# A feed-forward norm whose per-token scale moves behind the first product, with the tokens' parts made beside the output matrix, in a two-block model kernel on one core

## The reference, cut to what matters

```python
def rms_norm(x, g):
    y = xf * lax.rsqrt(jnp.mean(xf * xf, axis=-1, keepdims=True) + RMS_EPS)
    return (y * g.astype(jnp.float32)).astype(x.dtype)

def conv_glu_ffn(h, w_up, conv_w, w_down):
    up = causal_dwconv(h @ w_up, conv_w)          # three taps along the tokens, per channel
    gate, val = jnp.split(up, 2, axis=-1)
    return (jax.nn.silu(gate) * val) @ w_down     # D_FF = 2816

    # in first_block
    x = x + hybrid_mixer(...)                     # ends in: merged @ w_o
    h = rms_norm(x, ffn_norm_g[l])
    x = x + conv_glu_ffn(h, w_up[l], ffn_conv_w[l], w_down[l])
```

## Time and profile before

| what | us |
|---|---|
| runs | 1736.82, 1743.10, 1745.94 |
| median of the runs | 1743.10 |
| profiled execution, first to last instruction | 1743.0 |
| TensorE busy in it | 1663.4 (95%) |
| VectorE, ScalarE, GpSimd busy | 1147.6, 800.3, 347.2 |
| branch products (L933) begin | 301.86 |
| last product of the output matrix begins | 354.94 |
| first product of the feed-forward part (L1098) begins | 374.23 |
| last `down` ends, about | 565.2 |

### The profile page before, as it was taken

One profiled execution on the slowest core, in us unless ns is written; L12 is line 12 of the kernel. 1 busy time (PEld: TensorE's weight loads), 2 busy tenths in 40 slices (PEclk: granted clock), 3 DMA queues, 4 the chain that ended last, 5 costly groups with the idle time before them and its releaser, 6 DMA issues. The chain is left out here.

```text
span 1743.0 us, 32776 instructions
## 1 busy us (share of the span) xinstructions
PE 1663.4 (95%) x11200; PEld 1507.4 (86%) x11200; DVE 1147.6 (66%) x2258; ACT 800.3 (46%) x1331; POOL 347.2 (20%) x220
## 2 busy tenths in 40 slices
PE   4999998969999999999999998999999999999997
PEld 4987897859999977778999998999999888888886
DVE  4454423757777594661679994777775577777776
ACT  3442111345554463223355554555555455555554
POOL 0030000004444000335667995000000000000000
PEclk9999998989999999999999999999999999999999
DMA  6513222335554521114645786555556767666663
GB/s 229 191 39 108 75 87 98 132 120 181 185 188 169 195 86 49 49 37 172 203 152 187 221 230 190 178 178 172 179 177 201 227 231 239 232 231 229 235 238 123
DMA packets 92804, 289.44 MB, mean 166 GB/s; under 512 B 10304, under 2 KB 27072, under 8 KB 92352
## 3 DMA queue, kind: packets, MB, share of 16 engines
q1 hardware_dynamic: 92304, 287.61, 50.6%
q10 hardware_dynamic: 432, 0.90, 0.2%
HBM read 270.64 MB, written 17.83 MB: 166 GB/s over the span
## 5 line engine op out<-in xcount | busy, mean ns | idle before, releaser
L259 PE MATMUL psum<-arena_parts 128*128 128x256 f32 (+2 forms) x1664 | 477.2, 287 | 26.2 <-DVE ring_parts L254 12.3
L261 PE MATMUL psum<-arena_parts,ring_parts 128*128 128x256 f32 (+1 forms) x1600 | 450.4, 282 | 0.0
L2589 DVE TENSOR_TENSOR ring_parts<-ring,arena_parts 128x512 fp32r<-128x512 f32 x418 | 282.7, 690 | 122.5 <-ACT arena_parts L2389 98.8
L259 PEld LDWEIGHTS psum<-arena_parts 128*128 128x128 f32 x1664 | 316.0, 190 | 29.8 <-issue 22.0
L261 PEld LDWEIGHTS psum<-arena_parts,ring_parts 128*128 128x128 f32 x1600 | 303.6, 190 | 0.0
L260 PE MATMUL psum<-h_parts,arena_parts 128*128 128x256 f32 x1024 | 287.2, 280 | 0.0
L254 POOL TENSOR_TENSOR ring_parts<-ring,arena_parts 128x1024 fp32r<-128x1024 f32 x79 | 210.2, 2681 | 65.2 <-ACT arena_parts L250 48.0
L230 PE MATMUL psum<-h,ring 128*128 128x256 f32 x896 | 212.5, 397 | 0.0
L2358 PE MATMUL psum<-arena_parts,x_parts 128*128 128x512 f32 x512 | 206.1, 403 | 2.7 <-DVE x_parts L2616 2.7
L2360 PE MATMUL psum<-arena_parts,x_parts 128*128 128x512 f32 x512 | 202.7, 396 | 0.0
L2359 PE MATMUL psum<-ring_parts,x_parts 128*128 128x512 f32 x512 | 202.0, 395 | 0.0
(11 more groups left out here) (527 smaller groups left out, 2924.2 us busy)
## 6 DMA issues: line engine op xcount, KB each, us to landing
ring<-stream SPq DMA_DIRECT2D x473, 512.0 KB, 3.5
kept<-arena SPq DMA_DIRECT2D x128, 128.0 KB, 2.6
arena<-kept SPq DMA_DIRECT2D x32, 512.0 KB, 4.2
arena<-first SPq DMA_DIRECT2D x1, 2144.0 KB, 7.8
arena<-second SPq DMA_DIRECT2D x1, 1632.0 KB, 6.4
x<-x_t SPq DMA_DIRECT2D x1, 1024.0 KB, 5.7
out<-arena SPq DMA_DIRECT2D x4, 256.0 KB, 2.1
arena<-last ACTq DMA_DIRECT2D x1, 512.0 KB, 3.4
```

Of the source, the lines that this page charges most:

```text
L259: nc.tensor.matmul(dst, stationary[0], moving[0], start=first, stop=False)
L261: return nc.tensor.matmul(dst, stationary[1], moving[0], start=False, stop=last_one)
L2589: v.tensor_tensor(low[:, s, w], ring[:, s, w], expert_high[:, m % 2, w].bitcast(F32), ALU.subtract)\
```

## The change

- The merge and the feed-forward part are one block: no meeting of the engines between them, and none around a norm.
- While the output matrix is multiplied, as each tile of `x` is done, ScalarE makes `h_high` as the rounded `x` times the gain (no scale of the token) and the tile's square; VectorE makes `h_low` from `x`, the gain and `h_high` by one instruction (`x_low`). GpSimd adds the squares in pairs.
- TensorE multiplies by the identity straight behind the output matrix, then by ones, and goes on with `up`.
- The scale of the tokens is made while the first `up` runs. It is put on the products: `scale_up` multiplies a bank by `scale` into a new tile in SBUF, `up_scaled`, and `up_taken` says that the bank is free. `convolve` then reads `up_scaled`.
- The last two slots of `W_O` change places, so that slot 3, which `FF_FIRST` needs, comes free one block earlier.

```diff
-        W_O = (4, 5, 6, 7, 0, 1, 2, 3)
+        W_O = (4, 5, 6, 7, 0, 1, 3, 2)
...
+        up_scaled = a6.take(2, 2, T)
...
-        rms_norm(lambda k: x[:, k, :], lambda k: h[:, k, 0:T], "ffn_norm_g", RMS_EPS, squares,
-                 beside=(lambda act: [ff_high(act, n) for n in (-4, -3)], lambda dve: [ff_low(dve, n) for n in (-4, -3)]))
...
+                for k in range(KT):
+                    b = k % 4
+                    act.wait_ge(drained[b], ev_at.banks[b] + k // 4 + 4)
+                    nc.scalar.activation(h_high[:, k, :], x[:, k, :], ACT.Identity, scale=col("ffn_norm_g", k))\
+                        .then_inc(S("h_rounded"), 1)
+                    nc.scalar.activation(squares[:, k, 0:T], x[:, k, :], ACT.Square).then_inc(S("scalar_step"), 1)
+                    if k in (5, 6):
+                        ff_high(act, k - 9)
+                sca.n += KT
+                ff_high(act, -2)
...
+            @block.gpsimd
+            def _(pool):
+                for k in range(4):
+                    pool.wait_ge(S("scalar_step"), sca.n - 3 + k)
+                    nc.gpsimd.tensor_tensor(squares[:, 4 + k, 0:T], squares[:, 4 + k, 0:T], squares[:, k, 0:T], ALU.add)\
+                        .then_inc(S("norm_squares"), 1)
...
+                def x_low(k):
+                    dve.wait_ge(S("h_rounded"), split["h"] + k + 1)
+                    v.scalar_tensor_tensor(h_low[:, k, :], x[:, k, :], col("ffn_norm_g", k), h_high[:, k, :].bitcast(F32),
+                                           ALU.mult, ALU.subtract).then_inc(S("h_parts"), 1)
...
+                for k in range(4):
+                    pe.wait_ge(S("norm_squares"), normed["squares"] + k + 1)
+                    ins = mm(bank[7][:, 0:T], ones, squares[:, 4 + k, 0:T], start=k == 0, stop=k == 3)
+                ins.then_inc(S("norm_total"), 1)
...
-                        pe.wait_ge(S("up_read"), i * 2 + (j + 1))
+                        pe.wait_ge(up_taken, i * 4 + (2 * j + 2))
...
+                        if n + part == -1:
+                            pe.wait_ge(S("norm_mean"), n_norm + 1)
...
-                            src, dst, c = bank[4 + 2 * j + part], conv[:, j, part, :], i * 2 + (j + FT * part)
+                            src, dst, c = up_scaled[:, j, part, :], conv[:, j, part, :], i * 2 + (j + FT * part)
...
+                        v.tensor_tensor(up_scaled[:, j, part, :], bank[4 + 2 * j + part][:, 0:T], scale[:, 0:T], ALU.mult)\
+                            .then_inc(up_taken, 1)
...
+                dve.wait_ge(S("norm_total"), n_norm + 1)
+                vec.link(v.tensor_scalar(scale[:, 0:T], bank[7][:, 0:T], 1.0 / D, RMS_EPS, ALU.mult, ALU.add))
+                vec.tell(v.reciprocal(scale[:, 0:T], scale[:, 0:T]), S("norm_mean"), n_norm + 1)
+                ff_low(dve, -1)
+                dve.wait_ge(S("norm_root"), n_norm + 1)
                 with dve.Fori(0, pairs) as i:
                     for j in range(2):
                         ff_low(dve, 3 * j, i)
+                        scale_up(i, j)
                         ff_low(dve, 3 * j + 1, i)
                         convolve(i, j)
                         ff_low(dve, 3 * j + 2, i)
                 for j in range(2):
                     ff_low(dve, j, pairs)
                 for j in range(2):
+                    scale_up(pairs, j)
                     convolve(pairs, j)
```

More of the change, by code:

```diff
@@ L918, in build, with ff_block, ff_high, ff_low @@
         merged_sum, merged_rounded = S("gn_squares"), S("gn_inverse")
+        a6 = Area(arena)
+        conv = a6.take(2, 2, T)
+        hidden = a6.take(2, T)
+        up_scaled = a6.take(2, 2, T)
+        assert a6.at <= 4992
+        aux = Area(arena, 4992)
+        meta, meta_g, meta_squares = aux.take(KT, M), aux.take(KT, M), aux.take(KT, M)
+        both_g, both_square, eps_row = aux.take(KT), aux.take(KT), aux.take(1)
+        assert aux.at <= 5888
+        a6 = Area(arena, 5888)
+        sums_of = Area(arena, 20608).take(KT, P)
+        xp = Area(arena_parts[25344])
+        xn_block, xn_high, xn_low = xp.take(4, D), xp.take(KT, TT), xp.take(KT, TT)
+        a6p = Area(arena_parts[a6.at])
+        high, h_high = a6p.take(SLOTS, D), a6p.take(KT, T)
+        hid_high, hid_low = a6p.take(2, T), a6p.take(2, T)
+        h_low = h_parts[:, :, 0:T]
+        assert a6.at + a6p.at <= scratch_at
+        pairs = FT // 2 - 1
+        block_base, h_base = split["blocks"] + 8, split["h"]
+        before = {s: pe_at.rounds[s] + 2 for s in range(SLOTS)}
+        n_norm = normed["n"]
+        normed["n"] += 1
+        up_taken = S("up_taken")
+        def ff_block(n, i=0):
+            if n < 0:
+                return FF_FIRST[n + 4], before[FF_FIRST[n + 4]] + 1, block_base + n + 5
+            if isinstance(i, int) and i == pairs:
+                s = FF_LAST[n]
+                return s, before[s] + 1, block_base + 4 + 6 * pairs + n + 1
+            s = FF_SLOTS[n]
+            return s, i + (before[s] + (s in FF_FIRST) + 1), i * 6 + (block_base + 4 + n + 1)
+        def ff_high(act, n, i=0):
+            s, filled, number = ff_block(n, i)
+            act.wait_ge(full[s], filled * 16)
+            nc.scalar.activation(high[:, s, :], ring[:, s, :], ACT.Copy).then_inc(S("high"), 1)
+        def ff_low(dve, n, i=0):
+            s, filled, number = ff_block(n, i)
+            dve.wait_ge(S("high"), number)
+            nc.vector.tensor_tensor(low[:, s, :], ring[:, s, :], high[:, s, :].bitcast(F32), ALU.subtract)\
+                .then_inc(S("low"), 1)
+        xn_filled = [before[s] + (s in FF_FIRST) + pairs * (s in FF_SLOTS) + (s in FF_LAST) + 1 for s in range(4)]
+        def xn_part_high(act, n):
+            part_high(act, xn_block, n % 4, n // 4 + xn_filled[n % 4])
         with nc.Block() as block:
@@ L922, in _ @@
                 load(sp, range(4))
-                load(sp, range(4, 8))
-                load(sp, range(4))
+                load(sp, W_O[:4])
+                load(sp, W_O[4:])
                 load(sp, FF_FIRST)
@@ L1009, in _ @@
                 merged_lower(KT - 1)
[L1010 to L1060, removed]
@@ new lines, in _ @@
+                for k, s in enumerate(W_O):
+                    if k + 2 < KT:
+                        weights_low(k + 2)
+                    evacuate(dve, [s], [k % 4], 1, lambda _, b, i: v.tensor_tensor(
+                        x[:, k, :], x[:, k, :], b[:, 0:T], ALU.add))
+                    if k:
+                        x_low(k - 1)
+                ff_low(dve, -4)
+                x_low(KT - 1)
+                ff_low(dve, -3)
+                ff_low(dve, -2)
+            split["blocks"] += 8
@@ L1070, in _ @@
+            assert block_base == split["blocks"] and all(before[s] == pe_at.rounds[s] for s in before)
             @block.sync
@@ L1130, in tap, with scale_up @@
                     return par[:, bass.ds(c + (at["ffn_conv_w"] + 2 * FT * k), 1)]
-                def convolve(i, j):
-                    dve.wait_ge(S("ff_hidden"), i * 2 + (j + 1))
+                def scale_up(i, j):
                     for part in range(2):
@@ L1185, in silu @@
                     nc.scalar.activation(conv[:, j, 0, :], conv[:, j, 0, :], ACT.Silu).then_inc(S("ff_silu"), 1)
[L1187 to L1191, removed]
+                ff_high(act, -1)
+                nc.scalar.activation(spare[:], ones[:, 0:1], ACT.Sqrt)
+                act.wait_ge(S("norm_mean"), n_norm + 1)
+                nc.scalar.activation(scale[:, 0:T], scale[:, 0:T], ACT.Sqrt).then_inc(S("norm_root"), 1)
                 with act.Fori(0, pairs) as i:
@@ L1230, in build @@
             split["blocks"] += 3 * FT
-            split["h"] += 2
+            split["h"] += KT
+            normed["squares"] += 4
             for tiles in (pe_at, ev_at):
```

15 lines of the change are left out of this document (7 added, 8 removed).

## The result

The changed kernel takes 1731.51 us (median of 6 runs, 1726.52 to 1736.06) against 1742.55 for the kernel before in the same comparison; the ratio is 0.9942, with a 95% interval of 0.9922 to 0.9962. The forecast was 1730 in a range of 1722 to 1738, with a gain of 13.3 us; 11.0 were measured. Its profiled execution spans 1731.3 us.

What follows compares the result with a forecast made beforehand. TensorE, busy 95% of the span, was taken as the bound. Gains 13.7 + 2.9 - 2.7 + 0.2 gave 14.1, less 0.8 for the tail 13.3: 1743.0 - 13.3 = 1729.7, say 1730 us, range 1722 to 1738.

Steps and rivals of the forecast that it cites:

- Branch: TensorE's list ahead of the identity: one branch of four left, without a meeting; taken as 0.4 us, bounds zero and 0.81.
- Identity and ones: TensorE between output matrix and first `up`: products with the identity 3.6 us at full clock, with ones 1.9 us.
- Squares and low parts: Ahead of ones and first `up`: squares done by 358.3 at the latest, last `h_low` about 357.9; neither late.
- The wait at the first `up`: Entry to the loop: TensorE's 2.90 us wait goes, since the scale multiplications end at 370.8, before 372.3.
- the wait at the first `down`: Ahead of the loop's first `down`: a new wait of 2.7 us for `hide`, whose chain has not become shorter.
- The loop: Feed-forward loop: VectorE goes from 73.42 to about 83 of 100; with 4.0 us of steady slack, nothing counted.
- The slack of the second half: Loop's first two halves: slack between `hide` and `down` about 1 us, shorter than the steady loop's 4.0.
- The upper bound that rests on it: Loop's first two halves: a loss of at most 1.5 us, with nothing counted in the sum.
- The tail: Last convolution and `hide` ahead of the last `down`: 0.8 us lost, bounds 0.4 and 1.8.
- The rule of the Trainium skill that was weighed: VectorE instructions with two SBUF inputs share a port with GpSimd, one waits; taps reading `up_scaled` and `conv` join them.
- The rival that made of this a slower kernel: Convolution and `hide` block each other in every loop half, 5.6 us a half; 1762 us in all, chance 0.04.

Runs made afterwards that it cites:

- slots' run: Changed kernel with the first four `up` blocks in slots 4 to 7, freed first by the output matrix: 1724.94 us, ratio 0.9911 to the kernel before.
- scale done twice: Changed kernel with an extra multiplication of each bank by the token scale into a place nobody reads: 1725.56 us, ratio 0.9919 to the kernel before.
- taps' run: Changed kernel with the convolution reading the banks again and scaled products unread, so the tokens' scale is left out: 1729.15 us, ratio 0.9932 to the kernel before.
- slot order as before: Changed kernel with the last two slots of the output matrix in their old order: 1729.08 us, ratio 0.9944 to the kernel before.
- `up` waits for the root: Changed kernel with TensorE waiting for the root of the token scale ahead of its first `up`: 1733.63 us, ratio 0.9968 to the kernel before.

## Why the prediction was right, step by step

The stretch gained 12.8 us where the sum had 13.3, by these terms:

- *Branch:* 0.4 was taken between 0 and 0.81; the first identity product starts 0.12 behind the last of the output matrix, as any product does. It costs nothing: the lower bound.
- *Identity and ones:* 3.6 and 1.9 were taken, 3.43 and 1.54 it took to the start of what follows. The full clock was granted, as the windows show. By the reckoning of the prediction (the first product where the pace of the later ones puts it) `up` starts ahead by 14.4 us, not 13.7.
- *Squares and low parts:* none was late, as said. The low part of the last tile took 0.95 us instead of 0.48, beside GpSimd's last addition; it was done at 356.84 and wanted at 358.79 at the earliest, so it cost nothing.
- *The wait at the first `up`* went and *the wait at the first `down`* came: 2.7 was said, 2.35 and 2.47 measured. The slots' run shows its cause, the start of the reloads; the scale done twice shows that 0.8 of it was GpSimd's third step beside a low part. That the two waits are one is what the taps' run speaks for.
- *What the sum left out:* the clock behind that wait, 1.56 us. The sum had each wait at its length and no more, because behind 2.90 us in the same place before, and behind the 3.22 ahead of the ones, the products ran at full pace. This is the only term that was missing, and 1.4 of it were made up by what had been taken too dear: 0.7 up to the first `up`, 0.35 at this wait, 0.3 in the tail. That sum and stretch are only 0.5 us apart is therefore in part luck; these terms leave 0.2 unaccounted for.
- *The loop:* no product late, as said. VectorE came to 79.33 of 100, not 83, because a pair of first taps takes 0.61 us from SBUF where it took 0.87 from a bank, and two multiplications 0.75 where 0.84 was taken. The slack of the second half was not about 1 us, as the prediction has it: in the kernel before its `hide` ends at 400.74 and its `down` starts at 403.29. The upper bound that rests on it was not needed.
- *The tail:* 0.8 was said, 0.5 measured (0.79 waited, less the 0.27 before).

The rule of the Trainium skill that was weighed ("SBUF — State Buffer", section "Who interferes with whom") holds here for instructions with two inputs in SBUF, as the low parts beside `hide` and the 0.95 us above show. Of the taps the prediction told it too shortly. The second and third taps, which it had in mind, lie beside no step of GpSimd in the changed kernel and take 468 to 483 ns (in the kernel before, the row at 556.48 is of first taps, not of these). In the run with the slot order as before one of 88 starts together with a step (542.27) and takes 1027:

```profile
L1187 DVE SCALAR_TENSOR_TENSOR arena<-arena,par x88: 470/480/1027, 370.3 to 544.0; 128x255 f32<-128x255 f32 x44, 128x254 f32<-128x254 f32 x44
```

The first taps have one input tile in SBUF and were stretched all the same: the section exempts such an instruction only outside the modes that use both ports, and names `tensor_scalar` among those that can enter them. The lines of VectorE's first taps over all rounds (shortest, median, longest in ns), after:

```profile
L1184 DVE TENSOR_SCALAR arena<-arena,par x44: 336/348/893, 370.7 to 542.4; 128x256 f32<-128x256 f32 x44
```

and with the taps from the banks:

```profile
L1184 DVE TENSOR_SCALAR arena<-psum,par x44: 470/477/481, 371.2 to 543.5; 128x256 f32<-128x256 f32 x44
```

The reading from SBUF is faster alone and up to 893 ns beside GpSimd; that from a bank took 470 to 481 ns throughout. The rival that made of this a slower kernel needed 4.7 us of it in every half. In the steady loop `hide` and the convolution do not lie side by side, as said; they meet at the entry and in the tail (three first taps of 44), where the changed kernel's VectorE timeline shows a pair of first taps at twice its 0.61:

```profile
541.96 1.31 DVE L1184 TENSOR_SCALAR arena<-arena,par 128x256 f32<-128x256 f32 x2
```

That the whole program gained 11.0 and the stretch 12.8 is, in the profiled execution, the clock at other places (3.1 us in the next stage alone). For the medians this is only argued: no trace shows the rest for each run, and its spread over ten traces, 11 us, is larger than the difference.

## What to carry to other kernels

A norm's scale that is one number per token can go behind the product, and the product can start while the scale is still being made; but a meeting of engines behind the norm takes back the larger part, since it asks for all that was to lie beside the product (7.6 of 12.8 us here). When one wait goes, follow the chain that ended it to its end: if a later product of the same engine hangs on the same chain, the wait can come back there, and what helps is to start the chain earlier (here, first weights in the slots that come free first, another 3.5 us of the stretch). Judge such a change by the stretch that it touches, counted from a fixed instruction, where the rest of the program spreads by as much as the gain.

## What the runs showed of the hardware that was not expected

- A rest of TensorE of 2 to 3 us may or may not bring the clock down. Behind 2.35 us (378.49, the changed kernel) and 2.75 us (`up` waits for the root) it fell; behind 2.90 us in the kernel before (389.03) it did not, and behind 2.90 us at 373.90 (taps from the banks) it did. Behind 1.59 us (scale done twice) it stayed up. At one and the same place, the pause of the next stage, it fell in seven of ten traces behind 2.59 to 2.84 us and stayed up in three behind 2.66, 2.71 and 2.78. A fall cost 1.4 to 3.1 us, as much as the rest itself.
- More work on VectorE made the stretch shorter by 1.5 us: two more multiplications from a bank kept a low part away from GpSimd's third step, which took 0.73 us instead of 1.71.
- A branch in TensorE's list without a meeting cost nothing: the next product started 0.12 us behind the one before it.
